# The reciprocal root of two RMS norms, moved behind the projections that it scales

## What is computed

```python
def rms_norm(x, gain, eps=NORM_EPS):
    y = xf * lax.rsqrt(jnp.mean(xf * xf, axis=-1, keepdims=True) + eps)
    return y * gain

def swiglu(h, w_gate, w_up, w_down):
    return (jax.nn.silu(h @ w_gate) * (h @ w_up)) @ w_down

x = x + 0.5 * swiglu(rms_norm(x, ffn1_norm), ffn1_w_gate, ffn1_w_up, ffn1_w_down)
...                      # gated MLP mixer and differential attention, w_out
x = x + 0.5 * swiglu(rms_norm(x, ffn2_norm), ffn2_w_gate, ffn2_w_up, ffn2_w_down)
...                      # second block: state space model, window attention, convolutional FFN
```

## Time and profile before

| | |
|---|---|
| median of 3 runs | 1855.71 us (1854.34 to 1857.95) |
| time of the profiled execution | 1858.26 us |
| its span from first to last instruction | 1856.7 us |
| TensorE busy | 1828.9 us, 99% |
| VectorE, ScalarE, GpSimd busy | 55%, 39%, 9% |
| chain of waits, by engine | PE 93%, DVE 4%, ACT 2% |
| matmuls of the gate and up projections (L1876) | 3264, 41% of the chain |

### The profile page before, as it was taken

One profiled execution on the slowest core, in us unless ns is written; L12 is line 12 of the kernel. 1 busy time (PEld: TensorE's weight loads), 2 busy tenths in 40 slices (PEclk: granted clock), 3 DMA queues, 4 the chain that ended last, 5 costly groups with the idle time before them and its releaser, 6 DMA issues.

```text
span 1856.7 us, 23693 instructions
## 1 busy us (share of the span) xinstructions
PE 1828.9 (99%) x8907; PEld 1458.8 (79%) x8907; DVE 1027.0 (55%) x1433; ACT 728.8 (39%) x1019; POOL 168.8 (9%) x232
## 2 busy tenths in 40 slices
PE   8999999999999999999999999999998999999998
PEld 6888888877888677777787778887986788888887
DVE  6655436454563556555788733435586555555433
ACT  4222222233433887523332222224456355555322
POOL 3222001110000000004311020110000400000000
PEclk9999999999999999999999999999999999999999
DMA  6766422333322212222655552335122232222232
GB/s 207 239 214 212 142 80 77 96 124 105 98 71 91 69 46 69 68 91 79 210 171 148 136 160 79 94 99 182 60 78 68 70 112 90 90 90 79 91 91 79
DMA packets 171692, 206.79 MB, mean 111 GB/s; under 512 B 18404, under 2 KB 150114, under 8 KB 171106
## 3 DMA queue, kind: packets, MB, share of 16 engines
q1 hardware_dynamic: 144994, 161.97, 27.1%
q0 software_dynamic: 12640, 38.55, 6.6%
q10 hardware_dynamic: 13984, 5.27, 1.2%
HBM read 190.29 MB, written 17.56 MB: 112 GB/s over the span
## 4 chain that ended last, share of the span: by engine, by line
PE 93%; DVE 4%; ACT 2%; issue 0%; DMA 0%; ACTq 0%; DVEq 0%
PE bank L1876 41%; PE bank L1836 35%; PE bank L2101 6%; PE bank L1804 2%; PE bank L2203 1%; PE bank L2127 1%; DVE tmp L1152 1%; PE bank L1855 1%; DVE w_lo L1134 1%; DVE h_lo L1160 1%; PE bank L1896 1%; PE bank L2242 0%; PE bank L2138 0%; DVE h_lo L1162 0%; PE bank L1927 0%
## 5 line engine op out<-in xcount | busy, mean ns | idle before, releaser
L659 ACT CAST w_hi<-w_raw 128x2048 fp32r<-128x2048 f32 x158 | 301.0, 1906 | 824.5 <-PE bank L1876 442.2
L1134 DVE TENSOR_TENSOR w_lo<-w_raw,w_hi 128x2048 fp32r<-128x2048 f32 x157 | 370.5, 2360 | 455.1 <-ACT w_hi L659 454.9
L1876 PE MATMUL bank<-h_hi,w_hi 128*128 128x512 f32 x1088 | 432.2, 397 | 2.2 <-ACT h_hi L683 0.9
L1876 PE MATMUL bank<-h_hi,w_lo 128*128 128x512 f32 x1088 | 430.3, 396 | 0.0
L1876 PE MATMUL bank<-h_lo,w_hi 128*128 128x512 f32 x1088 | 342.2, 396 | 3.7 <-DVE h_lo L1160 2.3
L1876 PEld LDWEIGHTS bank<-h_hi,w_hi 128*128 128x128 f32 x1088 | 204.4, 188 | 54.3 <-issue 4.0
L1876 PEld LDWEIGHTS bank<-h_lo,w_hi 128*128 128x128 f32 x1088 | 204.1, 188 | 54.2 <-DVE h_lo L1160 3.1
L1876 PEld LDWEIGHTS bank<-h_hi,w_lo 128*128 128x128 f32 x1088 | 204.4, 188 | 48.5
L1836 PE MATMUL bank<-hid_hi,w_hi 128*128 128x512 f32 x528 | 208.8, 396 | 0.0
L1836 PE MATMUL bank<-hid_lo,w_hi 128*128 128x512 f32 x528 | 208.8, 396 | 0.0
L1836 PE MATMUL bank<-hid_hi,w_lo 128*128 128x512 f32 x528 | 208.8, 395 | 0.0
(11 more groups left out here) (416 smaller groups left out, 2433.1 us busy)
## 6 DMA issues: line engine op xcount, KB each, us to landing
w_raw<-in_w_in SPq DMA_DIRECT2D x29, 1024.0 KB, 5.1
mod_raw<-in_w_mod POOLq DMA_DIRECT2D x96, 256.0 KB, 3.8
w_raw<-in_ffn_w_gate SPq DMA_DIRECT2D x22, 1024.0 KB, 6.6
w_raw<-in_ffn_w_up SPq DMA_DIRECT2D x22, 1024.0 KB, 5.4
w_raw<-in_w_up SPq DMA_DIRECT2D x22, 1024.0 KB, 5.1
w_raw<-in_ffn_w_down SPq DMA_DIRECT2D x16, 768.0 KB, 4.8
w_raw<-in_ffn_w_down SPq DMA_DIRECT2D x16, 640.0 KB, 4.3
w_raw<-in_w_out SPq DMA_DIRECT2D x8, 1024.0 KB, 5.2
```

What stands on the lines that cost most here:

```text
L659: act.copy(w_hi[i % 2][:], w_raw[i % 2][:]).then_inc(S("w_hi_done"), 1)
L1134: dve.tensor_tensor(w_lo[s][:], w_raw[s][:], w_hi[s][:].bitcast(F32), ALU.subtract).then_inc(S("w_split"), 1)
L1876: mm = pe.matmul(bank[:], w[:, k, at], h[:, k, :], start=k == first and part == 0 and i == 0, stop=k == last and part == 1)
```

## The change

For ffn1 and ffn2 the projections no longer read normed tiles. ScalarE casts x times the gain straight to `h_hi` (`scaled_hi`), and VectorE makes `h_lo` from x, the gain and `h_hi` in one instruction (`scaled_lo`). The reciprocal root comes later: VectorE multiplies the gate's two banks with `rstd` into `tmp` before ScalarE takes the silu (`gate_scaled`, in every step), leaves the up banks as they are, and multiplies the down projection's banks with it before they are added to x.

The first gate panel is run in another order (`first_gate`): 32 matmuls with the high half of the weights, then the sums of squares, then 16 with the low half. The root's refinement stands within VectorE's first step: in ffn1 ahead of the modulation, in ffn2 behind it. At the start, GpSimd squares x and no longer splits a weight panel; VectorE splits panels 0 and 1 after the low halves of h; ScalarE casts them after all eight high halves. `n1`'s gain is loaded and turned by itself, ahead of x. Parameter rows and the bias product move between the two parts of the first gate panel, and with them the copy for which GpSimd's modulation DMAs wait. In ffn2 the idle products go as well, and `h_hi` and `h_lo` are made during the output projection. The norm before ffn3 is as before.

```diff
+            for k in range(KD):
+                wait_x(pool, "start", k)
+                if k >= 6:
+                    pool.wait_ge(S("norm_summed"), k - 5)
+                pool.tensor_tensor(tmp[:, k % 6, :], x[:, k, :], x[:, k, :], ALU.mult).then_inc(S("x_squared"), 1)
...
                 norm_cast(name, shift=shift)
+            def scaled_hi(name, before, gain, ks):
+                for k in ks:
+                    wait_x(act, before, k)
+                    act.activation(h_hi[:, k, :], x[:, k, :], ACT.Identity, scale=gain(k)).then_inc(S("norm_hi"), 1)
...
-                            act.wait_ge(S("pe_done"), i * 8 + (4 * base + 2 * t + 2))
-                            act.wait_ge(S("hid"), i * 2 + (HID[name] + t + 1))
-                            act.activation(tmp[:, t, :], B[t][:], ACT.Silu).then_inc(S("silu"), 1)
+                            act.wait_ge(S("gate_scaled"), i * 2 + (HID[name] + t + 3))
+                            act.activation(tmp[:, t, :], tmp[:, t, :], ACT.Silu).then_inc(S("silu"), 1)
...
-            norm("n1", x, lambda eng, k: wait_x(eng, "start", k), panel=1, between={4: 0})
+            done(act.activation(stat[:, 95:96], eps_col, ACT.Abs_reciprocal_sqrt))
+            act.wait_ge(S("x_turned"), 1)
+            scaled_hi("n1", "start", lambda k: gain1[:, k:k + 1], range(KD))
+            split(0)
+            split(1)
+            norm_root("n1")
...
-            norm("n2", x, lambda eng, k: wait_x(eng, "mixer", k), panel=BASE["ffn2"] + 1)
+            parts("w_out", lambda t: scaled_hi("n2", "mixer", lambda k: col("ffn2_norm", k), (t, )))
+            norm_squares("n2", x, lambda eng, k: wait_x(eng, "mixer", k))
+            split(BASE["ffn2"] + 1)
+            norm_root("n2")
...
+            def scaled_lo(name, gain, ks):
+                for k in ks:
+                    dve.wait_ge(S("norm_hi"), NORM[name] + k + 1)
+                    dve.scalar_tensor_tensor(h_lo[:, k, :], x[:, k, :], gain(k), h_hi[:, k, :].bitcast(F32), ALU.mult, ALU.subtract)                        .then_inc(S("norm_split"), 1)
...
                     with dve.Fori(start, stop) as i:
+                        if start == 0 and name == "ffn1":
+                            refined_root("n1")
                         if mods:
                             modulation(i + MOD_AT[name])
+                        if start == 0 and name == "ffn2":
+                            refined_root("n2")
                         if paired(extra):
                             prepared(extra, 0)
+                        for t in range(2):
+                            dve.wait_ge(S("pe_done"), i * 8 + (4 * base + 2 * t + 2))
+                            dve.wait_ge(S("hid"), i * 2 + (HID[name] + t + 1))
+                            dve.tensor_tensor(tmp[:, t, :], B[t][:], rstd[:], ALU.mult).then_inc(S("gate_scaled"), 1)
                         split(i * 2 + (base + 2), base)
...
-                            dve.scalar_tensor_tensor(x[:, k, :], down_bank(name, k)[:], factor(k), x[:, k, :], ALU.mult, ALU.add).then_inc(S(name + "_x"), 1)
+                            product = down_bank(name, k)[:]
+                            if name != "ffn3":
+                                product = tmp[:, 4 + k % 2, :]
+                                done(dve.tensor_tensor(product, down_bank(name, k)[:], rstd[:], ALU.mult))
+                            dve.scalar_tensor_tensor(x[:, k, :], product, factor(k), x[:, k, :], ALU.mult, ALU.add).then_inc(S(name + "_x"), 1)
...
+            dve.wait_ge(S("x_t"), 1)
+            dve.tensor_copy(gain1[:], B[6][:, 0:KD]).then_inc(S("x_turned"), 1)
+            for k in range(KD + 3):
+                if k < KD:
+                    dve.wait_ge(S("x_t"), k + 2)
+                    dve.tensor_copy(x[:, k, :], B[2 + k % 4][:]).then_inc(S("x_turned"), 1)
+                if k >= 3:
+                    scaled_lo("n1", lambda k: gain1[:, k:k + 1], (k - 3, ))
+            split(0)
+            split(1)
...
-            norm("n2", x, lambda k: col("ffn2_norm", k), panel=BASE["ffn2"] + 1)
+                scaled_lo("n2", lambda k: col("ffn2_norm", k), (2 * i, 2 * i + 1))
+            split(BASE["ffn2"] + 1)
...
-            def gate_up(name, h_name, free):
+            def first_gate(n, banks, h_name, between):
+                wh, wl = panel(w_hi, n, KD, PC), panel(w_lo, n, KD, PC)
+                pe.wait_ge(S("w_hi_done"), n + 1)
+                for k in range(KD):
+                    for wait, h in ((ready_hi, h_hi), (ready, h_lo)):
+                        wait(h_name)(k)
+                        for t, bank in enumerate(banks):
+                            pe.matmul(bank[:], wh[:, k, t * P:(t + 1) * P], h[:, k, :], start=k == 0 and h is h_hi, stop=False)
+                between()
+                pe.wait_ge(S("w_split"), n + 1)
+                for k in range(KD):
+                    for t, bank in enumerate(banks):
+                        mm = pe.matmul(bank[:], wl[:, k, t * P:(t + 1) * P], h_hi[:, k, :], start=False, stop=k == KD - 1)
+                        if k == KD - 1:
+                            mm.then_inc(S("pe_done"), 2)
+            def gate_up(name, h_name, free, sums=None):
                 base = BASE[name]
                 for start, stop, mods, extra in PHASES.get(name, ((0, GU_STEPS, False, None),)):
                     with pe.Fori(start, stop) as i:
                         for half in range(2):
+                            if sums and start == 0 and half == 0:
+                                first_gate(base, [B[0], B[1]], h_name, sums)
+                                continue
                             pe.wait_ge(S("w_split"), i * 2 + (base + half + 1))
                             free(i, half)
...
+                    pe.wait_ge(S("gate_scaled"), HID[name] + KF + 2)
...
+            norm("n1", range(6))
...
+            def first_sums():
...
+                norm("n1", (6, 7))
...
+            gate_up("ffn1", "n1", swiglu_free("ffn1"), first_sums)
...
-            norm("n2")
-            idle_products(9, x[:, 0, 0:2 * P])
-            gate_up("ffn2", "n2", silu_free("ffn2"))
+            wait_x(pe, "mixer", 5)
+            gate_up("ffn2", "n2", swiglu_free("ffn2"), lambda: norm("n2"))
```

97 lines of the change are left out of this document (47 added, 50 removed), and 2 rows, old and new, of the table ROWS.

## The result

The changed kernel took 1826.43 us (median of 4 runs, 1825.67 to 1830.45) against 1855.98 us (4 runs): ratio 0.9843, 95% interval 0.9831 to 0.9854. It is 29.6 us faster, 1.6%; the forecast was 1858.5 us, with 1853.5 as the low end of the range.

What follows compares the result with a forecast made beforehand. TensorE was taken as the bound, with VectorE late next at both second steps. Terms -4.0 + 2.0 + 0.75 + 1.5 + 2.5 = +2.75 us on the median 1855.71 gave 1858.5 us, range 1853.5 to 1862.

Steps and rivals of the forecast that it cites:

- The first step: Whole kernel: TensorE busy 99%, 96-matmul steps stay 22.50 us, so only its few waits can change the time.
- start, second step: First FFN: VectorE's low weight half sets the second step, 45.9 instead of 49.9; 4.0 us won, between 1.0 and 5.0.
- start, clock: First FFN's start: no clock fall in the sum; one in the 1.9 us wait named only as an aside.
- two last x: Last x of each FFN's down projection: another 0.70 us and a hand-over on the path, twice; 1.5 us lost.
- second FFN, second step: Second FFN: modulation data don't move, VectorE bounds; second step 904.2 against 902.2, 2.0 us lost, between 1.6 and 3.0.
- second FFN, clock: Second FFN's new wait: clock falls, second gate panel partly at 1.2 GHz; 2.5 us lost, between 0 and 3.4.
- its later steps: Second FFN's later steps: scalings before each low half exceed the cover in two steps; 0.75 us lost.
- The first gate matmul: First FFN's start: copies, low halves, casts and 1 us of contention put it at 17.6; without contention 17.0.
- rival C: Start: GpSimd's squares and VectorE's low halves block each other in full, 3 us more; +5.75, 1861.5 us; chance 0.16.

Runs made afterwards that it cites:

- the weights moved instead: The changed kernel with an unused 32-byte tile ahead of w_hi and another behind w_lo; 1863.11 us.
- The kernel with the loads sooner: The changed kernel with GpSimd's first four modulation loads issued right behind its squares (ffn1) and behind the last x (ffn2); 1819.39 us.
- the changed kernel's second profile: The changed kernel run once more, unaltered, beside the kernel before with 32 unused bytes on one chip; 1827.74 us.
- the fill: The changed kernel with 32 idle products (20 and 12) in the two TensorE waits of the second FFN's first step; 1828.03 us.
- The padded kernel before: The kernel before with one unused 32-byte tile behind `mod`, where the changed kernel has `gain1`; 1816.46 us, 1816.44 when run again.

## Why the prediction was wrong, step by step

**The first step failed.** The forecast said that the change takes away no 96-product step, so "a change is worth only what it takes out of, or puts into, the few places where TensorE waits". That took the 22.50 us of a step as given. It was not: 32 bytes where `gain1` stands, and nothing else, changed it to 21.93 us and the time by 40 us, against which all other terms are small. No rival had it. The allocation was in the kernel of after, and so was the fact that it stands ahead of the rows' tiles; what was missing was the question whether the steady pace itself can move.

**The other terms** can be judged between kernels of the slow pace: before, and the changed kernel with 32 bytes more, whose median was 6.8 us above. The forecast for that was +2.75, with +6.3 as the upper end of the range, so even there it was too low. Its rows, from the timelines:

```profile
28.86 2.57 POOL L562 DMA_DIRECT2D mod_raw<-in_w_mod  x4 [0.94 <-POOL zero L574]
...
34.74 0.49 DVE L1304 TENSOR_SCALAR mod_acc<-mod_raw,small 128x512 f32<-128x512 f32 x1 [2.09 <-DMA mod_raw<-in_w_mod]
...
48.17 0.79 PE L1920 MATMUL bank<-h_hi,w_hi 128*128 128x512 f32 x1 [2.06 <-DVE w_lo L1146]
...
889.39 0.49 DVE L1304 TENSOR_SCALAR mod_acc<-mod_raw,small 128x512 f32<-128x512 f32 x1 [12.25 <-DMA mod_raw<-in_w_mod]
...
904.37 0.80 PE L1920 MATMUL bank<-h_hi,w_hi 128*128 128x512 f32 x1 [1.88 <-DVE w_lo L1146]
...
1271.12 0.69 DVE L1372 SCALAR_TENSOR_TENSOR x<-tmp,x 128x512 f32<-128x512 f32 x1
```

```profile
48.10:72.60 24.50, 24.43 (x99) 19.64 (x99) 14.93 (x19) 4.54 (x6) 5.59 (x10) 0.92 0.81 265
...
904.30:929.00 24.70, 24.63 (x99) 19.74 (x99) 19.31 (x30) 4.63 (x6) 4.30 (x8) 0.91 0.55 175
```

| term | forecast | measured |
|---|---|---|
| start, second step | -4.0 (45.9) | -1.6 (48.17 against 49.76; with the weights moved instead, 47.26) |
| start, clock | 0 | +1.8 (step of 24.4 against 22.6) |
| two last x | +1.5 | +0.73 each |
| second FFN, second step | +2.0 (904.2) | +1.2 (904.37; 1.0 of it came from ahead) |
| second FFN, clock | +2.5 | +2.0 |
| its later steps | +0.75 | +0.6 and +0.5 |
| sum | +2.75 | +6.0 |

- **Start, mis-sized.** The step was "the DMA stands at 29 and lands at 32.4 to 33.4". It was issued at 28.86 and its first tile used at 34.74: 5.9 us, where I had 3.4 to 4.4, around the median of 3.8 over all 96 loads. The group then took 9.8 us, with 2.5 of waiting for its own tiles, where I had 9.15. In the changed kernel the median of the loads that lay between 14 and 46 us was 6.0 (before: 4.3), beside two weight panels of 1 MB that took 8.6 and 8.8 us (before: 10.7 and 5.3). The kernel with the loads sooner began its modulation right behind the root, without the 2.46 us of waiting, and won 3.3 us (45.82 against 49.09; 1.5 against the 47.30 of the changed kernel's second profile), which shows that the late data were the main cause; why the loads took longer is open. The first gate matmul was right: 17.6 forecast, 17.45 here. (The working itself had arrived at 18.0 with 1 us of contention, and then took 17.6.)
- **The clock at the start** I had put into rival C as an aside and not into the sum. TensorE waited here in two pieces, between the up panel's end near 43.1 and 48.17, with the modulation's small products between them, and the clock fell at 45.2 (the small products' starts go from 0.11 to 0.21 us apart).
- **Rival C's own mechanism** was there, but at 1.4 us instead of 4. VectorE's low halves of h and GpSimd's squares took turns:

```profile
8.35 1.57 DVE L1161 SCALAR_TENSOR_TENSOR h_lo<-x,gain,h_hi 128x512 fp32r<-128x512 f32 x1
...
13.33 0.92 DVE L1161 SCALAR_TENSOR_TENSOR h_lo<-x,gain,h_hi 128x512 fp32r<-128x512 f32 x1
...
13.67 2.93 POOL L571 TENSOR_TENSOR tmp<-x 128x512 f32<-128x512 f32 x2
```

  Apart from each other a low half took 0.74 us and a square 1.04. Here each of the first six low halves ended 0.54 to 0.56 us after the end of the square that was running, and a square that met one took 1.48. So the low half that began with a square waited it out (1.57), while those that began late in one lost 0.18 each (0.92). The four ahead of the last copy lost 1.4 us together; I had taken 1. The Trainium skill, "SBUF — State Buffer", section "Who interferes with whom", has an exclusive lock between the two engines there: by that rule, the trace agrees. My reading of it, that each low half would wait a whole square, was the wrong part.
- **Second FFN, right in mechanism, and mis-sized.** VectorE bounds it, and late data start it. The times look exact, 889.3 forecast and 889.39 measured for the modulation, 904.2 and 904.37 for the next step, but that is luck: 1.0 us of them came from ahead, which the forecast had left out of these times. Without it the loss is 1.2 us, below my 1.6 to 3.0, since the first tile was used 3.1 us after the first issue (886.30) and not 3.5. The loads that stand ahead are 20, not sixteen as I had written.
- **The clock there, right**: 2.0 us, forecast 2.5, and the fill showed that the idle time is its cause. The Trainium skill, "TensorE: Matmul & The Clock Gate", section "HAM oscillation — how this bites in real kernels", has an idle gap put the next work on the low clock: by that rule, the trace agrees, 24.0 against 22.0 us.
- **Down projections, right**: 1271.12 against 1265.03, of which 0.73 arose there.
- **Later steps, right in kind**, 1.1 instead of 0.75.

The profiled runs differ by 4.8 us and not 6.0, since before lost 3.4 us to a fall of the clock at 1343.3 that the other had not. At the last copy of the output the difference is 3.1 (1854.81 against 1851.72); 1.7 more stand behind it, ahead of the end of the program, and I have no cause for them. The padded kernel before had a low clock too, for 3.4 us from 1370.9, so such a fall doesn't hang on the edits.

At the fast pace the same edits cost 10 to 11 us, more than at the slow one. TensorE comes to its waits sooner, and VectorE's chain and the DMAs don't: the first FFN's second step, won by 1.6 us at the slow pace, starts 0.3 later here (49.09 against 48.81 in the padded kernel before); in the second FFN the second step lost 2.1 beyond what came from ahead (887.51 against 882.97, of which 2.4 came from ahead), instead of 1.2, and two later steps 2.2 instead of 1.1.

## What to carry to other kernels

Where an edit adds or resizes any on-chip tile, compare the distance between the start addresses of the two tiles that the main matmul reads, and the pace of an untouched block, before reading anything into the total; an unused tile of the same size is the control that parts the two. When TensorE is busy 99% of the span, a few ns on each matmul can outweigh all waits together: here 6.3 ns on 6,650 of them (41.6 us) against 27.8 us of idle time. And where work is opened up ahead of a VectorE chain, move the issue of that chain's data first, every slot of it: here the last load issued set the gain, not the first.

## What the runs showed of the hardware

- Matmuls of 128x128 by 128x512 (fp32r) in the down projection's steady row started 226.7 ns apart in the kernels where the two operands' tiles stood a multiple of 256 bytes from each other in the partition, and 233.4 where they were 32 bytes off either way; 64 and 128 off lay between (228.9 and 232.4).
- The attention's 128-column fp32 products had the same mean in both kernels (275 ns). Their two tiles moved together, so their distance did not change; whether it would matter to them is not shown.
- With one tile off of three, products that don't read it took 232.3 and 239.3 ns to the next start, and the one that does 228.4.
- Loads of 256 KB took 3.8 us in the median of the kernel before. Between 14 and 46 us, with two 1 MB panels under way, the median was 4.3 before and 6.0 after.
- A VectorE instruction with two inputs in SBUF and GpSimd's squares of SBUF tiles took turns: 0.74 us alone, 1.57 when begun with a square, 0.92 when begun 0.37 us before a square's end.
